# Banded attention: first query and key tiles from one weight chunk, second key tile later

## What is computed

```python
proj = rmsnorm(x) @ w_in                   # q: 16 heads of 64, k: 4 heads, v: 4 heads
q, k = rope(q, positions), rope(k, positions)
scores = q @ k.T * 64 ** -0.5              # |key - query| <= 128 only, blocks of 128 queries
m = maximum(max(scores), sink)             # one sink per query head
p = exp(scores - m)
out = p @ v / (sum(p) + exp(sink - m))     # 4 query heads share a k and a v head
x = x + out @ w_out
```

## Time and profile before

| | us |
|---|---|
| median of three executions | 1437.6 |
| lowest and highest | 1435.58, 1437.78 |
| the profiled execution | 1437.62 |
| its span | 1435.8 |
| TensorE busy in the span | 1403.9 |
| VectorE busy | 945.3 |
| ScalarE busy | 704.2 |
| GpSimd busy | 110.3 |

### The profile page before, as it was taken

How to read it: one execution, slowest core, us unless ns; L and a number is a source line. 1 busy time by engine, 2 the same in 40 slices (tenths; PEclk the granted TensorE clock), 3 DMA queues, 4 the chain that set the end, 5 groups by cost and what they waited for, 6 DMA issues and landing times.

```text
span 1435.8 us, 21052 instructions
## 1 busy us (share of the span) xinstructions
PE 1403.9 (98%) x8006; PEld 1191.1 (83%) x8006; DVE 945.3 (66%) x1939; ACT 704.2 (49%) x1409; POOL 110.3 (8%) x172
## 2 busy tenths in 40 slices
PE   9999999999999999999999999998899999999998
PEld 8777766887888888898899988766578898899987
DVE  6566664566577668784489745768567784388743
ACT  6655543355544353552356533667643563266533
POOL 0111001000000000100111000001000110011000
PEclk9999999999999999999999999999999999999999
DMA  6211111123222131542566332212021553466422
GB/s 252 88 60 59 60 59 59 45 99 110 71 91 74 59 117 63 147 122 95 151 158 156 107 128 80 102 51 78 31 88 60 152 119 121 118 165 159 125 86 73
DMA packets 44372, 144.99 MB, mean 101 GB/s; under 512 B 5297, under 2 KB 7985, under 8 KB 37361
## 3 DMA queue, kind: packets, MB, share of 16 engines
q1 hardware_dynamic: 34624, 126.61, 26.5%
q0 software_dynamic: 9216, 16.78, 6.9%
q10 hardware_dynamic: 432, 0.27, 0.1%
HBM read 138.78 MB, written 2.23 MB: 98 GB/s over the span
## 4 chain that ended last, share of the span: by engine, by line
PE 91%; DVE 4%; ACT 2%; DMA 1%; issue 1%; SPq 0%; DVEq 0%; POOLq 0%; POOL 0%; ACTq 0%
PE PS L708 89%; PE PS L999 1%; PE PS L727 1%; DVE WL L1389 1%; DVE FT L1389 1%; DVE FT L1909 0%; DMA FT<-in_pos 0%; DMA FT<-rows 0%; DMA FT<-FT 0%; ACT XH L1081 0%; ACT WH L1081 0%; DVE FR L1389 0%; SPq L2089 0%; PE PS L975 0%; ACT FT L1081 0%
## 5 line engine op out<-in xcount | busy, mean ns | idle before, releaser
L1389 DVE TENSOR_TENSOR WL<-RAW,WH 128x512 fp32r<-128x512 f32 (+1 forms) x452 | 294.2, 675 | 102.0 <-ACT WH L1081 101.6
L708 PE MATMUL PS<-FR,WH 128*128 128x512 f32 (+1 forms) x1132 | 339.9, 383 | 4.9 <-DVE WL L1389 2.2
L708 PE MATMUL PS<-XH,WH 128*128 128x512 f32 (+1 forms) x952 | 341.0, 358 | 0.9 <-ACT VF L1081 0.9
L708 PE MATMUL PS<-XH,WL 128*128 128x512 f32 (+1 forms) x952 | 331.2, 348 | 0.0
L1081 ACT ACTIVATE WH<-RAW 128x512 fp32r<-128x512 f32 (+1 forms) x452 | 263.8, 613 | 136.7 <-PE PS L708 121.2
L708 PE MATMUL PS<-XL,WH 128*128 128x512 f32 (+1 forms) x952 | 330.5, 347 | 0.0
L708 PEld LDWEIGHTS PS<-FR,WH 128*128 128x128 f32 x1132 | 208.4, 188 | 46.7 <-issue 3.4
L708 PE MATMUL PS<-FR,WL 128*128 128x512 f32 (+1 forms) x566 | 216.0, 382 | 0.0
L708 PEld LDWEIGHTS PS<-XH,WH 128*128 128x128 f32 x952 | 180.3, 189 | 28.2 <-issue 6.5
L708 PEld LDWEIGHTS PS<-XH,WL 128*128 128x128 f32 x952 | 180.1, 189 | 23.4
L708 PEld LDWEIGHTS PS<-XL,WH 128*128 128x128 f32 x952 | 180.5, 190 | 21.0 <-issue 1.0
(11 more groups left out here) (150 smaller groups left out, 1846.6 us busy)
## 6 DMA issues: line engine op xcount, KB each, us to landing
RAW<-in_f_in SPq DMA_DIRECT2D x64, 256.0 KB, 5.0
RAW<-in_f_in SPq DMA_DIRECT2D x32, 512.0 KB, 4.1
RAW<-in_w_in SPq DMA_DIRECT2D x12, 1024.0 KB, 4.8
RAW<-in_m_in SPq DMA_DIRECT2D x12, 1024.0 KB, 4.8
RAW<-in_f_in SPq DMA_DIRECT2D x12, 1024.0 KB, 4.8
RAW<-in_f_oa SPq DMA_DIRECT2D x16, 768.0 KB, 4.6
RAW<-in_f_ob SPq DMA_DIRECT2D x16, 640.0 KB, 3.9
RAW<-in_f_in POOLq DMA_DIRECT2D x32, 256.0 KB, 5.1
```

Of the source, the lines that this page charges most:

```text
L708: return e.matmul(o, l, r, start=start, stop=stop, skip_group_check=True)
L1389: return e.tensor_tensor(o, a, b, op)
```

## The change

The columns of the attention's input weights are put in another order: chunk 0 holds the first key tile and the first query tile, chunk 2 the second query tile and the second key tile. So x=0 is key tile 0, x=1 and x=2 are the query tiles of pair 0, and x=3 is key tile 1, which only pairs 2 and 3 read. `a_slot` gives each tile the FR slot that it had, and the factor -0.125 of queries follows the tiles. The turns of pair 0 wait for the tiles that they read, and their places count from `seen[2]`.

```diff
-    when = [seen[3] + 4 + n for n in range(8)] + [seen[5] + 3 + n // 2 for n in range(8)]
+    when = [seen[2] + 4 + n for n in range(8)] + [seen[5] + 3 + n // 2 for n in range(8)]
...
     def a_slot(x):
-        return 2 * x
+        return 2 * (0, 2, 3, 1)[x] if x < 4 else 2 * x
...
-            p.wait_ge("ropr", 4 + 2 * pr)
+            p.wait_ge("ropr", 4 + 2 * pr if pr else 2 + g)
             p.wait_ge("scev", 48 + 2 * n)
-            q, k = a_slot(2 + 2 * pr + g), a_slot(pr // 2)
+            q, k = a_slot(2 + 2 * pr + g if pr else 1 + g), a_slot(3 * (pr // 2))
...
-                copy(FT[:, 2 + T.i % 2, :], b, scale=1.0 if T.i < 2 else -0.125).then_inc(sems["rope1"], 1)
+                copy(FT[:, 2 + T.i % 2, :], b, scale=1.0 if T.i in (0, 3) else -0.125).then_inc(sems["rope1"], 1)
...
-        "a_in": pack(aw, list(range(12))),
+        "a_in": pack(aw, [0, 4, 2, 3, 5, 1, 6, 7, 8, 9, 10, 11]),
```

## The result

| | before | after |
|---|---|---|
| median of nine executions, us | 1438.92 | 1443.79 |
| lowest and highest, us | 1435.58, 1441.07 | 1441.42, 1445.42 |
| span of the profiled execution, us | 1435.8 | 1442.9 |

The ratio after to before is 1.0034, with a 95% interval of 1.0022 to 1.0045. The forecast was 1442.3 within 1438.7 to 1445.0, 4.7 us over the kernel before; the medians lie 4.9 us apart. (The kernel before has a higher median with nine executions than it had with three, and single executions of it differ by over 5 us, the slower ones at a lower mean clock of TensorE: among those timed beside e5 to e8, 1434.55 us at 0.995 and 1440.44 us at 0.991. So ratios are worth more here than times. Where a difference in us stands beside an interval, both are the ratio times the median of the kernel before.)

The account below looks back on a forecast made before the run. TensorE, busy 1403.9 of 1435.8 us, was taken as the bound, with pairs 0 and 1 starting behind x=3 and x=5. A 3.1 us stall plus a 1.6 us clock fall on 1437.6 gave 1442.3, range 1438.7 to 1445.0.

Parts of the forecast that it names:

- The wait that takes the place of the old one: Pair 0's start: a1(0) loses its 0.59 us wait, but TensorE pauses 3.0 us at a1(1) for VectorE's reductions.
- a4(7): Before x=5's eviction: this unit of pair 0 now runs ahead of it and delays it by 1.1 us.
- the mixes' 0.45: VectorE between x=5's rotation and split: mix 17's split is done earlier, so a1(8) gains 0.45 us.
- TensorE's pause in front of a1(8): Start of pair 1: TensorE's own work ends near 951.6, a1(8) starts at 952.8; a 1.1 us pause, already counted.
- e3's sum of +0.1: Way to a1(8) if VectorE takes a1(0) at once: −0.59 + 1.1 − 0.45 = +0.1 us, from the faster rival, chance 0.07.
- The stall part alone, 3.1: Delay of a1(8) without any clock fall: 2.4 us lost at a1(1), plus 1.1, minus 0.45, rounded to +3.1 us.
- The clock: TensorE behind the a1(1) pause: one short fall to about half clock, charged 1.6 us, bounds 0 and 3.2.
- The long form of the fall: TensorE's clock behind the pause: low twice as long, 3.2 us instead of 1.6; chance 0.11.
- the second rival: Clock fall twice as long, or one more in front of pair 1: 1437.6 + 3.1 + 3.2 = 1443.9, up to 1445; chance 0.11.
- without a pause: Faster rival at a1(1): VectorE takes a1(0) at once, and the long clock fall behind a1(8) might vanish: 1434.5; chance 0.07.
- without a fall: Rival behind the a1(1) pause: the stall costs 3.1 us but the clock stays up: 1440.7; chance 0.22.
- Absorbed: Rival for 990 to 1040: TensorE's idle 6.65 us swallows 2 to 3 us of delay: 1437.6 to 1438.8; chance 0.15.

Follow-up runs that it names:

- e5: Changed kernel with mix 16 and mix 17 back at 32 and 33, as in the kernel before; one execution, read by trace only: x=5's eviction to a1(8) 8.34 us.
- e8: Kernel before with only pair 1's turns spread, one a step instead of two, old pairing kept; 1434.47 us, ratio 0.9983 to the kernel before.
- e3: Changed kernel with x=3's rotation and split moved behind pair 0's a1 on VectorE; 1438.34 us, ratio 1.0007 to the kernel before.
- e1: Changed kernel with the new pairing of columns and tiles, but pair 0's turns at their old places, counted from seen[3]; ratio 1.0002 to the kernel before.
- e2: Kernel before, old pairing, with only pair 0's turns two steps earlier (seen[3] + 2); 1443.94 us, ratio 1.0049 to the kernel before.
- e6: The e3 kernel with a4(7) behind step 31 again, mix 16 at 32 and mix 17 at 34.25; 1437.12 us, ratio 0.9998 to the kernel before.
- e4: Changed kernel with 12 unused matmuls of 128x512 filling TensorE's pause in front of a1(1); ratio 1.0018 to the kernel before.

## Why the prediction was right

**The wait that takes the place of the old one.** It was put at a1(1), released by VectorE's reduction at 914.05, 3.0 us long. It is there, released at 914.99, 3.53 us long. The half microsecond is not in the mechanism: SyncE begins to issue x=3's four swaps 1.05 us behind x=3's last matmul in both kernels, but the four issues stretch over 3.73 us here and over 3.14 before, so the last of them lands later and VectorE waits 3.04 us instead of 2.45. e5, with the same order around it, has 3.32 us of issues and a pause of 3.12 us. e3 shows that VectorE's list is the cause, and e1 and e2 that the pairing is not.

**Terms at x=5.** a4(7) at 1.1 us measured 0.98 (e6 against e3), the mixes' 0.45 measured 0.41 (8.34 - 7.93, e5) to 0.52 (8.45 - 7.93). TensorE's pause in front of a1(8), 1.1 in the sum, is 1.17. e3's sum of +0.1 came out as +0.04. The stall part alone, 3.1, measured 2.8 in e4, where VectorE waited only 2.21 us for the swaps, 0.24 less than in the kernel before.

**The clock.** It was put at 1.6 us for one short fall; the clock of 0.56 over 3.50 us loses 3.50 × 0.44 = 1.5, and filling the pause gave back 1.5 (e4). So the pause is charged once as a wait and once more as slow matmuls. The rule on long idle gaps in the Trainium skill, "TensorE: Matmul & The Clock Gate", section "Why this matters for your kernels", agrees with this trace: 0.56 behind 3.53 us. The long form of the fall, which had a chance of 0.11, did occur in two of the three profiles with such a pause (e2 and e5), so 0.11 looks low. That the changed kernel's own profile has the short form is luck in part; which form its other executions had is not known.

**Together**: 3.1 + 0.6 (the late swaps) + 1.5 = 5.2 us against 5.15 in the profile, and 4.7 against 4.9 in the medians. As a bare time, 1443.8 lies nearer to the second rival's 1443.9 than to the forecast's 1442.3; that is the base, whose median is 1438.9 with nine executions where the sum started from 1437.6. By the traces, the rivals without a pause, without a fall, and with a fall of twice the length did not come true in the profiled execution. "Absorbed" fails on the other half of the span: from a1(8) to its end it is 486.1 us before and 487.7 after, and 486.3 to 487.0 in e1 to e4 and e6; nothing that is lost in front of a1(8) is given back behind it.

**Slips in the working.** Three slips move the forecast by less than 0.1 us: a1(0) follows the fourth step of v tiles, 48 matmuls, and not the eighth; it waits for two splits fewer and not one (`ropr` 2 in place of 4); and 3.60 × 0.43 is 1.55, put down as 1.6.

**What stays open.** Why the low clock begins sooner and lasts longer in e2 and e5 than in the changed kernel's profile was not followed further, nor was a version tried in which pair 0 starts still earlier.

## What to carry to other kernels

Moving work earlier on the engine that bounds gains only if its consumer can be earlier as well. Look at the list of the in-order engine that frees the buffer: what stands ahead of that release, and until when does it wait? Here a tile that nobody needed yet stood ahead of that release, with its DMA wait, its rotation and its split, and set the time of everything behind it. The repacked weights alone made the kernel slower; they only made it possible to move those entries back, and that took the loss away (e3). And look for dependent turns that stand next to each other: with one dense step between the turns of pair 1 the kernel before gained 2.65 us (e8), while the new pairing at its best gained nothing measurable (e6).

## What was not expected of the hardware

Twelve matmuls without a purpose (2.91 us) took 1.5 us off the way by keeping the granted clock at 1.00 (one trace each, e4 and the changed kernel). In e2 the same sort of pause (3.35 us) was followed by matmuls of 256 columns every 0.22 us at once, in the changed kernel by some at 0.12 first and near half clock only from about 916.4 on. The low stretch is also of two lengths: 0.56 over 3.50 us in the changed kernel, 0.51 over 6.80 us in e2 and over 7 us in e5. So what a pause costs beyond itself differs between profiles with nearly the same pause (3.12 to 3.53 us).
